# A hybrid conv/RWKV-7 layer on one core: another table of dense steps, and a y that is read from PSUM twice instead of copied

## The chip, the core and the metric

One NeuronCore of a Trainium2 chip runs the whole layer. TensorE (PE) multiplies, VectorE (DVE) and ScalarE (ACT) do the elementwise work, GpSimd (POOL) a few masks and some DMA issues, SyncE (SP) issues the other DMAs. The metric is the device time of one execution in microseconds (us); lower is better. The kernel before takes 2533.69 us (median of three runs, 2532.3 to 2533.92).

## The reference

One layer on 512 tokens and 16 meta tokens (T = 528) with width 2048, all in float32:

```
h = rms_norm(h_res, g);  p = h @ w_in
y_conv = short_conv(p[:, :3072])            # 8 tiles of 128 channels
r, k, v, decay, a, gate = token_shift(p[:, 3072:], mu), ...
S_t = S_{t-1} * w_t + (S_{t-1} a_t) b_t^T + v_t k_t^T;   y_t = S_t r_t    # per head of 64
y = (y - mean(y)) * rsqrt(var(y) + eps) * lnx_w + lnx_b
y_rwkv = (y + sum(r * k * r_k) * v) * g
h_res += concat(y_conv, y_rwkv) @ w_out
h_res += square(relu(rms_norm(h_res) @ w_up)) @ w_down
out = rms_norm(h_res)[16:]
```

## The kernel before, in words

Every large product is made of "dense steps": for one 128-row slice of the contraction, three matmuls (high part of the weights by high and low part of the activations, low part of the weights by high part). ACT casts each raw block of weights to its high part (`split`, L663), DVE subtracts to get the low part (`split`, L920); four dense steps use one such block.

The RWKV heads are worked in 8 pairs of two heads. The first seven pairs are one loop (PE L1506, ACT L820, DVE L1180), the last stands behind it. One pair has two strands that PE interleaves: 96 dense steps that make the projections of conv tiles and of the next pair's r, k, v (six tiles of 16 steps; 48 in the last pair), and the pair's own chain of small steps in chunked form. Each step of the chain has a name: ss (sum of squares of the key), low (decay and rate), vtr, gram0, tr, gram1, amv, base1 and base2 (DVE inverts 16x16 blocks, which SP carries through DRAM and back), x16, t16, x32, tt32 (the inverse is doubled), pq, gh, y0, z2 to z8 (the state is passed from chunk to chunk), y, and var. `PACE` (L70) says how many dense steps PE does ahead of each named step; `schedule` adds them up, and for the last pair caps them at 48. All three engines walk the same table: at each name ACT and DVE do that step's part (`steps_of`) and then the weight splits that are due (one per four dense steps), or, for the names in SPLIT_FIRST (L133: low, base1, base2, x16, y, var), the splits first. Engines meet by three counters (`pe_done`, `act_done`, `dve_done`); `dve("rt")` in PE's code is a wait until DVE has done its step rt.

The part that the change touches most, at a pair's end: PE's y adds the last term into PSUM banks 2 and 3 of PW. ACT squares them into ysq (sqc, L788) and copies them to SBUF (yk into ybuf, L789). PE's var puts the head means of the squares into bank 0 and the gate product into bank 1. ACT takes the square root (std, L792), DVE the reciprocal (inv2, L1133), multiplies ybuf by it (y1, L1134), applies weight and bonus (y2, L1136) and multiplies by the gate in bank 1 (y4, L1137). The next pair begins with kk on DVE (L1000), a square on ACT (sq, L742) and on PE ss (L1354), which writes banks 2 and 3 again.

Of the kernel before, what the change touches and what calls it, by code (L numbers as in the profile page):

```python
# [28 lines left out]
ALU = mybir.AluOpType  # L29
# [6 lines left out]
SEQ = 512  # L36
# [30 lines left out]

PACE = dict(ss=2, low=5, vtr=5, ahead0=6, gram0=8, tr=2, gram1=3, base1=0, base2=0, amv=2, ahead1=4, ahead2=4,  # L70
            ahead3=4, ahead4=5, ahead5=4, x16=3, t16=2, x32=2, tt32=2, pq=2, gh=3, y0=5, z2=4, z3=2, z4=1, z5=2, z6=1,
            z7=2, z8=2, y=2, var=3, ahead6=4)

PE_STEPS = [n for n in PACE if n[:4] != "base" and n[:5] != "ahead"]
Z_STEPS = ("z2", "z3", "z4", "z5", "z6", "z7", "z8")
ACT_STEPS = ["for_sqrt", "sq", "nrm", "for_sig", "sigw", "siga", "for_exp", "vtok", "epv", "em", "ep", "gs", "ghi", "btok",
             "ktok", "bonb", "atok", "mv", "x16", "x32", "warm", "pq", "sqc", "yk", "std"]
DVE_STEPS = (["kk", "ssm", "inv", "ld", "scan", "mid", "mu", "epv", "gs", "kkn", "tfac", "kp",
              "at", "b", "bt", "rt", "kt", "rb", "gram0", "bon", "glo", "gram1", "diag"]
             + [f"{s}{m}" for m in (2, 4, 8) for s in ("pr", "ar", "pl", "al")] + ["ut"]  # L80
# [25 lines left out]
def at(static, per=0, it=0):  # L106

    return it * per + static


def step(steps, name, it):

    return at(steps.index(name) + 2, len(steps), it)
# [9 lines left out]
def schedule(last):  # L123
    pace, total = [], 0
    for n in PACE.values():
        total += n
# [13 lines left out]

Y_FROM = list(PACE).index("x16")

# [21 lines left out]
def hybrid_layer(nc, x, meta, norm_mix_g, w_in, shift_mu, conv_w, decay_w0, decay_w2, iclr_a0, iclr_a2,  # L164
# [85 lines left out]
    warm = m_sb("warm", [P, 1])  # L250
    uni = m_sb("uni", [P, 9 * T])
    ld, mu, ep, em, epv, asig, kk, kp, fsq = (uni[:, i * T:(i + 1) * T] for i in range(9))
    W = SLOTS * C
# [3 lines left out]
    INV = by_chunk(0, 2).rearrange("p m c n -> p (m c) n")  # L257
    PROD_AT = 10 * W
    PQ = uni[:, 0:4 * W].rearrange("p (h c n) -> p h c n", h=2, c=SLOTS)
    ybuf = uni[:, 4 * W:4 * W + SEQ]  # L260
    ycen = uni[:, 4 * W + SEQ:4 * W + 2 * SEQ]
    low_g, low_g2 = em, epv[0:TAIL]
    ET = uni[:, 4 * W + 2 * SEQ:4 * W + 3 * SEQ]
    ysq = uni[:, 0:SEQ]
# [60 lines left out]
    def halves(ap):  # L325
        return ap.rearrange("p (a n) -> p a n", a=2)
# [8 lines left out]
    def token_order(ap):  # L335

        return ap.rearrange("p (k a n) -> p a k n", a=2, n=C)

    def by_bank(b):

        return PW[:, b:b + 2, 0:4 * C].rearrange("p a (k n) -> p a k n", n=C)

    def in_row(i):

        return PW[:].rearrange("p a n -> p (a n)")[:, i * TP:(i + 1) * TP]

    def turned(b):

        return PW[:, b:b + 2, :].rearrange("p a n -> p (a n)")[:, 0:TP]

    def pw(b):
        return PW[:, b:b + 2, 0:HALF]
# [288 lines left out]
    def _(act):  # L641
# [83 lines left out]
        def pair(j, last=False):  # L725
            n_done = [0]

            def done(name, ins):
                assert ACT_STEPS[n_done[0]] == name, (name, ACT_STEPS[n_done[0]])
                n_done[0] += 1  # L730
                ins.then_inc(act_done, 1)
                own(name)

            pe = lambda name: act.wait_ge(pe_done, step(PE_STEPS, name, j))
            dve = lambda name: act.wait_ge(dve_done, step(DVE_STEPS, name, j))
# [3 lines left out]
            def steps_of(name):  # L739
                if name == "ss":  # L740
                    done("for_sqrt", nc.scalar.activation(warm[:], eps_t[:, 0:1], ACT.Sqrt))
                    done("sq", nc.scalar.activation(fsq, zk[:], ACT.Square, scale=feat("k_k")))  # L742
                    dve("ssm")
                    done("nrm", nc.scalar.activation(fsq, fsq, ACT.Sqrt))
                    done("for_sig", nc.scalar.activation(warm[:], eps_t[:, 0:1], ACT.Sigmoid))
                if name == "low":
                    pe("low")
                    done("sigw", nc.scalar.activation(halves(ld), pw(0), ACT.Sigmoid, bias=feat("w0")))
                    done("siga", nc.scalar.activation(halves(asig), pw(2), ACT.Sigmoid, bias=feat("a0")))
                    done("for_exp", nc.scalar.activation(warm[:], eps_t[:, 0:1], ACT.Exp))  # L750
                if name == "vtr":
                    pe("vtr")
                    done("vtok", nc.scalar.copy(v_tok[:].rearrange("p c n -> p (c n)"), turned(0)))
                    dve("epv")
                    done("epv", nc.scalar.activation(epv, epv, ACT.Exp))
                    done("em", nc.scalar.activation(em, mu, ACT.Exp, scale=-1.0))
                    done("ep", nc.scalar.activation(ep[:, 0:SEQ], mu[:, META:T], ACT.Exp))
                    dve("gs")
                    done("gs", nc.scalar.activation(gs[:], gs[:], ACT.Exp))
                if name == "ahead0":  # L760
                    act.wait_ge(g_loaded, at(64, 64, j))
                    nc.scalar.copy(g_hi[:], g_w[:])
                    done("ghi", nc.scalar.copy(g_tail[:], g_w2[:]))
                if name == "tr":
                    pe("tr")
                    done("btok", nc.scalar.copy(b_tok[:].rearrange("p c n -> p (c n)"), in_row(0)))
                    done("ktok", nc.scalar.copy(k_tok[:].rearrange("p c n -> p (c n)"), in_row(1)))
                    dve("bon")
                    done("bonb", nc.scalar.activation(bonus[:], bonus[:], ACT.Identity, bias=feat("lnb")))
                if name == "amv":  # L770
                    pe("amv")
                    done("atok", nc.scalar.copy(AMV[:, :, :, 0:HS], PW[:, 2:4, 0:W].rearrange("p h (c n) -> p h c n", c=SLOTS)))
                    done("mv", nc.scalar.copy(AMV[:, :, :, HS:P], PW[:, 0:2, 0:W].rearrange("p h (c n) -> p h c n", c=SLOTS)))
                if name in ("x16", "x32"):
                    pe(name)
                    b = 2 if name == "x16" else 0
                    done(name, nc.scalar.copy(XM[:, :, 1:, :].rearrange("p h c n -> p h (c n)"), PW[:, b:b + 2, C:W]))
                if name == "tt32":

                    done("warm", nc.scalar.activation(warm[:], eps_t[:, 0:1], ACT.Sqrt))  # L780
                if name == "pq":
                    pe("pq")
                    for h in range(2):
                        ins = nc.scalar.copy(PQ[:, h, :, :].rearrange("p c n -> p (c n)"), turned(2 * h))
                    done("pq", ins)
                if name == "y":
                    pe("y")
                    done("sqc", nc.scalar.activation(token_order(ysq), by_bank(2), ACT.Square))  # L788
                    done("yk", nc.scalar.copy(token_order(ybuf), by_bank(2)))  # L789
                if name == "var":  # L790
                    pe("var")
                    done("std", nc.scalar.activation(ysq, PW[:, 0, :], ACT.Sqrt, bias=eps_t[:, 1:2]))  # L792

            splits, tiles, y_split = 0, 0, 0
            for i, (name, k) in enumerate(zip(PACE, schedule(last))):

# [96 lines left out]
    def _(dve):  # L893

        V = nc.vector
# [85 lines left out]
        def pair(j, last=False):  # L981
            n_done = [0]

            def done(name, ins):
                assert DVE_STEPS[n_done[0]] == name, (name, DVE_STEPS[n_done[0]])
                n_done[0] += 1
                ins.then_inc(dve_done, 1)
                own(name)
# [8 lines left out]
            def steps_of(name):  # L997
# [133 lines left out]
                if name == "var":  # L1131
                    act("std")
                    done("inv2", V.reciprocal(ysq, ysq))  # L1133
                    done("y1", V.tensor_tensor(ycen, ybuf, ysq, ALU.mult))  # L1134
                    act("bonb")
                    done("y2", V.scalar_tensor_tensor(ycen, ycen, feat("lnw"), bonus[:], ALU.mult, ALU.add))  # L1136
                    done("y4", V.tensor_tensor(bt[:, PAD + META:TP], ycen, PW[:, 1, :], ALU.mult))  # L1137
# [19 lines left out]
            splits, tiles, y_split = 0, 0, 0  # L1157
            for i, (name, k) in enumerate(zip(PACE, schedule(last))):
                if name not in SPLIT_FIRST:
# [112 lines left out]
    def _(pe):  # L1272
# [62 lines left out]
        def pair(j, last=False):  # L1335
            n_done = [0]

            def done(name, ins):
                assert PE_STEPS[n_done[0]] == name
                n_done[0] += 1  # L1340
                ins.then_inc(pe_done, 1)

            act = lambda name: pe.wait_ge(act_done, step(ACT_STEPS, name, j))
            dve = lambda name: pe.wait_ge(dve_done, step(DVE_STEPS, name, j))
# [5 lines left out]
            def steps_of(name):  # L1350
                if name == "ss":
                    act("sq")
                    for a in range(2):
                        ins = M(PW[:, 2 + a, 0:HALF], same_head[:], half(fsq, a), start=True, stop=True)  # L1354
                if name == "low":
# [138 lines left out]
            k_steps = 0  # L1494
            for name, k in zip(PACE, schedule(last)):
                while k_steps < k:
# [96 lines left out]
```

## Time and profile before

| | us |
|---|---|
| median of three runs | 2533.69 |
| the profiled execution | 2533.69 |
| its span | 2532.2 |
| PE busy | 2441.7 (96%) |
| DVE busy | 1133.7 (45%) |
| ACT busy | 794.5 (31%) |

The span runs from the first to the last instruction of the profiled execution, and its own time is 1.5 us longer. PE's busy time counts matmuls that overlap as one. A pair takes about 98 us, the eight stand between about 114 and 900 us. Where a row says "idle before <- X", the engine had nothing to do until X was done; "issue" means that no releaser was seen.

### The profile page before, as it was taken

Reading aid. Unit: us, or ns where it says so; the run is one execution under the profiler, and the core shown is the slowest. Engines: PE = TensorE matmul, PEld = TensorE weight load, DVE = VectorE, ACT = ScalarE, POOL = GpSimd, SP = SyncE. Lnnn points to the kernel's source line nnn. Section 1 sums busy time; section 2 is a strip of 40 time slices with the busy share of each in tenths; the row PEclk is TensorE's granted clock in tenths of the full one; section 3 lists DMA queues with packets and bytes.
Section 4 is the critical chain, followed back from the end, with each engine's and each line's share of the span. In section 5 each row is a group of like instructions: output and inputs, shape, how many; then the busy total and the mean of one; then the engine's idle time right before and its main releaser. Section 6 shows DMA issues by size and latency. Waiting matters only on the chain.

```text
span 2532.2 us, 44221 instructions
## 1 busy us (share of the span) xinstructions
PE 2441.7 (96%) x16510; PEld 2062.2 (81%) x16510; DVE 1133.7 (45%) x1725; ACT 794.5 (31%) x1333; POOL 177.2 (7%) x207
## 2 busy tenths in 40 slices
PE   6999999999999789999999999999999999999997
PEld 6988888889889568888888888888888888888886
DVE  6357566476576554443333333333333333333343
ACT  6334333344344222232232232232232222221333
POOL 4001001010010022200000000000000000000033
PEclk8999999999999889999999999999999999999999
DMA  8242432342432453333323233223333333332332
GB/s 210 75 91 74 96 88 74 93 94 67 97 84 79 107 156 93 89 94 108 92 83 108 86 88 108 87 87 108 88 102 91 89 102 91 90 100 83 100 92 92
DMA packets 507783, 242.87 MB, mean 96 GB/s; under 512 B 102976, under 2 KB 500672, under 8 KB 507136
## 3 DMA queue, kind: packets, MB, share of 16 engines
q1 hardware_dynamic: 502672, 226.63, 32.9%
q0 software_dynamic: 4992, 14.43, 1.7%
q8 instruction: 102, 1.67, 0.3%
q14 instruction: 17, 0.14, 0.0%
HBM read 224.08 MB, written 16.92 MB: 95 GB/s over the span
## 4 chain that ended last, share of the span: by engine, by line
PE 85%; DMA 5%; DVE 4%; SPq 2%; ACT 2%; issue 2%; ACTq 0%; DVEq 0%
PE PD L1320 63%; PE PD L1323 16%; DMA w_raw<-in_w_in 2%; DMA gram<-NA 1%; DMA inverse<-UU 1%; DMA UU<-gram 1%; PE PW L1429 1%; SPq L387 1%; PE PW L1474 1%; DVE uni L1082 0%; DVE w_lo L920 0%; DVE uni L1076 0%; DMA x_rows<-in_x 0%; DVE act_lo L925 0%; PE PW L1436 0%
## 5 line engine op out<-in xcount | busy, mean ns | idle before, releaser
L920 DVE TENSOR_TENSOR w_lo<-w_raw,w_hi 128x512 fp32r<-128x512 f32 x780 | 555.9, 750 | 312.9 <-ACT w_hi L663 304.9
L663 ACT CAST w_hi<-w_raw 128x512 fp32r<-128x512 f32 x780 | 455.9, 619 | 730.1 <-PE PD L1320 484.5
L1320 PE MATMUL PD<-act_hi,w_hi 128*128 128x512 f32 x1408 | 557.6, 396 | 8.3 <-DVE act_lo L978 8.3
L1320 PE MATMUL PD<-act_lo,w_hi 128*128 128x512 f32 x1408 | 558.6, 397 | 0.0
L1320 PE MATMUL PD<-act_hi,w_lo 128*128 128x512 f32 x1408 | 555.6, 395 | 0.0
L1320 PE MATMUL PD<-u_hi,w_hi 128*128 128x512 f32 x1024 | 409.7, 400 | 0.0
L1320 PE MATMUL PD<-u_hi,w_lo 128*128 128x512 f32 x1024 | 403.3, 394 | 0.0
L1320 PE MATMUL PD<-u_lo,w_hi 128*128 128x512 f32 x1024 | 401.5, 392 | 0.0
L1320 PEld LDWEIGHTS PD<-act_hi,w_hi 128*128 128x128 f32 x1408 | 265.6, 189 | 73.3 <-DVE act_lo L978 9.2
L1323 PE MATMUL PD<-act_hi,w_hi 128*128 128x264 f32 x1376 | 298.9, 299 | 20.0 <-DVE act_lo L925 10.5
L1320 PEld LDWEIGHTS PD<-act_hi,w_lo 128*128 128x128 f32 x1408 | 266.1, 189 | 60.4
L1320 PEld LDWEIGHTS PD<-act_lo,w_hi 128*128 128x128 f32 x1408 | 265.2, 188 | 60.7 <-issue 0.2
L1323 PE MATMUL PD<-act_lo,w_hi 128*128 128x264 f32 x1376 | 281.1, 286 | 0.0
L1323 PE MATMUL PD<-act_hi,w_lo 128*128 128x264 f32 x1376 | 280.8, 286 | 0.0
L1255 DVE TENSOR_TENSOR res<-PD,res 128x512 f32<-128x512 f32 x128 | 88.5, 692 | 413.6 <-PE PD L1320 413.6
L1323 PEld LDWEIGHTS PD<-act_hi,w_hi 128*128 128x128 f32 x1376 | 214.2, 190 | 36.7 <-issue 23.6
L1320 PEld LDWEIGHTS PD<-u_hi,w_lo 128*128 128x128 f32 x1024 | 192.2, 188 | 50.1
L1320 PEld LDWEIGHTS PD<-u_lo,w_hi 128*128 128x128 f32 x1024 | 192.2, 188 | 45.1
L1320 PEld LDWEIGHTS PD<-u_hi,w_hi 128*128 128x128 f32 x1024 | 192.2, 188 | 43.7
L1323 PEld LDWEIGHTS PD<-act_lo,w_hi 128*128 128x128 f32 x1376 | 214.5, 189 | 0.0
L1323 PEld LDWEIGHTS PD<-act_hi,w_lo 128*128 128x128 f32 x1376 | 214.2, 189 | 0.0
L1239 DVE SCALAR_TENSOR_TENSOR nt<-PD,rs 128x512 f32<-128x512 f32 x64 | 44.3, 692 | 366.1 <-PE PD L1320 365.9
(263 smaller groups left out, 1475.8 us busy)
## 6 DMA issues: line engine op xcount, KB each, us to landing
w_raw<-in_w_up SPq DMA_DIRECT2D x256, 256.0 KB, 3.1
w_raw<-in_w_down SPq DMA_DIRECT2D x256, 256.0 KB, 2.9
w_raw<-in_w_in SPq DMA_DIRECT2D x200, 256.0 KB, 3.4
w_raw<-in_w_out SPq DMA_DIRECT2D x64, 256.0 KB, 2.8
x_rows<-in_x SPq DMA_DIRECT2D x4, 1024.0 KB, 8.2
residual<-res POOLq DMA_DIRECT2D x2, 2048.0 KB, 12.0
out<-rows SPq DMA_DIRECT2D x8, 512.0 KB, 4.9
uni<-inverse SPq DMA_DIRECT2D x16, 240.0 KB, 4.2
```

What stands on the lines that cost most here:

```text
L387: sp.dma_start(w_raw[:, q % RAW, :, first:first + width], src).then_inc(raw_loaded[q % RAW], 16)
L663: nc.scalar.copy(w_hi[:, q % RING], w_raw[:, q % RAW]).then_inc(hi_split, 1)
L920: V.tensor_tensor(w_lo[:, q % RING], w_raw[:, q % RAW], w_hi[:, q % RING].bitcast(F32), ALU.subtract).then_inc(lo_split, 1)
L1239: V.scalar_tensor_tensor(nt1[:, m % 3, :], pd_seq(n), 0.0, rs1[:], ALU.max, ALU.mult).then_inc(evacuated[n % 2], 1)
L1255: V.tensor_tensor(res[:, m, :], pd_seq(n), res[:, m, :], ALU.add).then_inc(evacuated[n % 2], 1)
L1320: ins = M(pd_seq(n), w, v[:, k, first:first + SEQ], start=begin, stop=end)
L1323: ins = M(PD[:, 2 * (n % 2) + a, 0:HALF], w, v[:, k, a * HALF:(a + 1) * HALF], start=begin, stop=end)
L1429: ins = M(PW[r, 2 + h, k * C:(k + 1) * C], XM[r, h, k, :], TTM[r, h, k, :], start=True, stop=True)
L1474: ins = M(PW[:, (c - 1) % 2, 0:P], GT[:, c - 1, :], HB[:, 0, :] if c == 1 else ZB[:, c - 2, :], start=True, stop=True)
```

## The change

The table PACE is another one (still 96 steps in sum); ahead6, which had 4 steps behind var, is gone, and amv stands ahead of base1 and base2. In cumulative dense steps: gram0 comes at 24 (26 before), gram1 at 29 (31), amv at 31 (33), x16 at 54 (57), t16 56 (59), x32 59 (61), pq 64 (65), gh 67 (68), y0 72 (73), z2 to z8 at 76, 78, 80, 82, 84, 86, 88 (77, 79, 80, 82, 83, 85, 87), y 91 (89), var 96 (92). ACT no longer copies y (yk); y1 reads it from PSUM. PE waits for kk ahead of ss.

```diff
-PACE = dict(ss=2, low=5, vtr=5, ahead0=6, gram0=8, tr=2, gram1=3, base1=0, base2=0, amv=2, ahead1=4, ...
-            ..., z7=2, z8=2, y=2, var=3, ahead6=4)
+PACE = dict(ss=2, low=4, vtr=5, ahead0=6, gram0=7, tr=2, gram1=3, amv=2, base1=0, base2=0, ahead1=2, ...
+            ..., z7=2, z8=2, y=3, var=5)
@@ ACT_STEPS
-             "ktok", "bonb", "atok", "mv", "x16", "x32", "warm", "pq", "sqc", "yk", "std"]
+             "ktok", "bonb", "atok", "mv", "x16", "x32", "warm", "pq", "sqc", "std"]
@@
-    ybuf = uni[:, 4 * W:4 * W + SEQ]
@@ ACT, name == "y"
                     done("sqc", nc.scalar.activation(token_order(ysq), by_bank(2), ACT.Square))
-                    done("yk", nc.scalar.copy(token_order(ybuf), by_bank(2)))
@@ DVE, name == "var"
                     done("inv2", V.reciprocal(ysq, ysq))
-                    done("y1", V.tensor_tensor(ycen, ybuf, ysq, ALU.mult))
+                    done("y1", V.tensor_tensor(token_order(ycen), by_bank(2), token_order(ysq), ALU.mult))
@@ PE, name == "ss"
                     act("sq")
+                    dve("kk")
                     for a in range(2):
                         ins = M(PW[:, 2 + a, 0:HALF], same_head[:], half(fsq, a), start=True, stop=True)
```

PE at the end of the loop's body and the start of the next pair, before. The rows end with ss; PW is the PSUM of the small steps, PD that of the dense ones, and var's matmuls stand four dense steps further up:

```order
L1323 MATMUL PD<-act_hi,w_lo 128x264 x2
L1506 REGISTER_ALU
L1506 COMPARE_AND_BRANCH
L1323 MATMUL PD<-act_hi,w_hi 128x264 [waits lo_split,evacuated0]
L1323 MATMUL PD<-act_hi,w_hi 128x264
L1323 MATMUL PD<-act_lo,w_hi 128x264 x2
L1323 MATMUL PD<-act_hi,w_lo 128x264 x2
L1323 MATMUL PD<-act_hi,w_hi 128x264 x2
L1323 MATMUL PD<-act_lo,w_hi 128x264 x2
L1323 MATMUL PD<-act_hi,w_lo 128x264 x2
L1354 MATMUL PW<-uni,same_head 128x264 [waits pair_steps_act]
```

The same place on PE in the changed kernel (lines are two less, from L1353 on one less):

```order
L1488 MATMUL PW<-low_tail,g_tail 128x512
L1505 REGISTER_ALU
L1505 COMPARE_AND_BRANCH
L1321 MATMUL PD<-act_hi,w_hi 128x264 [waits lo_split,evacuated0]
L1321 MATMUL PD<-act_hi,w_hi 128x264
L1321 MATMUL PD<-act_lo,w_hi 128x264 x2
L1321 MATMUL PD<-act_hi,w_lo 128x264 x2
L1321 MATMUL PD<-act_hi,w_hi 128x264 x2
L1321 MATMUL PD<-act_lo,w_hi 128x264 x2
L1321 MATMUL PD<-act_hi,w_lo 128x264 x2
L1353 MATMUL PW<-uni,same_head 128x264 [waits pair_steps_dve,pair_steps_act]
```

The last matmul of var now stands directly ahead of the branch, and ss waits for DVE's counter as well as for ACT's.

DVE at the same place, from y4 to the first step behind ss, before:

```order
L1137 TENSOR_TENSOR bt<-uni,PW 128x512 [waits pair_steps_dve]
L993 REGISTER_ALU
L919 REGISTER_ALU [waits pair_steps_dve]
L920 TENSOR_TENSOR w_lo<-w_raw,w_hi 128x512 [waits hi_split]
L1180 REGISTER_ALU
L1180 COMPARE_AND_BRANCH
L1000 TENSOR_SCALAR uni<-zk,par 128x528 [waits z_done]
L1002 TENSOR_SCALAR uni<-PW 128x528 [waits pair_steps_pe,pair_steps_dve]
```

and now:

```order
L1135 TENSOR_TENSOR bt<-uni,PW 128x512 [waits pair_steps_dve]
L991 REGISTER_ALU
L1178 REGISTER_ALU [waits pair_steps_dve]
L1178 COMPARE_AND_BRANCH
L998 TENSOR_SCALAR uni<-zk,par 128x528 [waits z_done]
L1000 TENSOR_SCALAR uni<-PW 128x528 [waits pair_steps_pe,pair_steps_dve]
```

The weight split between y4 and the branch is gone (it stands ahead of the reciprocal), so the branch comes directly behind the wait for y4.

ACT in front of the copy that t16 waits for (L777, of PE's x16), before, from the cast of the third last block on:

```order
L662 REGISTER_ALU [waits raw_loaded3]
L663 CAST w_hi<-w_raw 128x512 [waits quarter_used]
L660 REGISTER_ALU
L662 REGISTER_ALU [waits raw_loaded0]
L663 CAST w_hi<-w_raw 128x512 [waits quarter_used]
L662 REGISTER_ALU [waits raw_loaded1]
L663 CAST w_hi<-w_raw 128x512 [waits quarter_used]
L734 REGISTER_ALU
L777 COPY uni<-PW 128x2x256 [waits pair_steps_pe]
```

and now:

```order
L661 REGISTER_ALU [waits raw_loaded3]
L662 CAST w_hi<-w_raw 128x512 [waits quarter_used]
L659 REGISTER_ALU
L661 REGISTER_ALU [waits raw_loaded0]
L662 CAST w_hi<-w_raw 128x512 [waits quarter_used]
L733 REGISTER_ALU
L776 COPY uni<-PW 128x2x256 [waits pair_steps_pe]
```

The cast of the block in raw_loaded1 has moved behind the copy.

## Rows read from the trace of the kernel before

**Rows 1.** The page: busy time of the engines, PE's granted clock in 40 slices.

```profile
PE 2441.7 (96%) x16510; PEld 2062.2 (81%) x16510; DVE 1133.7 (45%) x1725; ACT 794.5 (31%) x1333; POOL 177.2 (7%) x207
...
PEclk8999999999999889999999999999999999999999
```

**Rows 2.** Waits of PE, whole span: line, releaser, us in total, times, longest.

```profile
PE PW L1410 <- DMA uni<-inverse: 8.2, 4, 7.3
PE PW L1418 <- ACT uni L777: 7.9, 8, 1.1
PE PW L1354 <- ACT uni L742: 6.4, 8, 2.2
...
PE PW L1392 <- DVE KA L1038: 2.9, 8, 0.4
```

**Rows 3.** PE's timeline at a boundary: start, duration, instruction, [idle before <- releaser].

```profile
404.05 0.39 PE L1489 MATMUL PW<-low_tail,g_tail 128*128 128x512 f32 x1
404.28 0.40 PE L1323 MATMUL PD<-act_hi,w_hi 128*128 128x264 f32 x2
...
406.96 0.40 PE L1323 MATMUL PD<-act_hi,w_lo 128*128 128x264 f32 x2
409.12 0.50 PE L1323 MATMUL PD<-act_hi,w_hi 128*128 128x264 f32 x2 [1.76 <-issue]
...
410.43 0.40 PE L1323 MATMUL PD<-act_hi,w_lo 128*128 128x264 f32 x2
411.11 1.16 PE L1354 MATMUL PW<-uni,same_head 128*128 128x264 f32 x4 [0.28 <-ACT uni L742]
```

**Rows 4.** ACT's timeline at the same boundary.

```profile
404.48 0.69 ACT L792 ACTIVATE uni<-PW,eps_t 128x512 f32<-128x512 f32 x1 [2.23 <-PE PW L1489]
...
408.69 1.28 ACT L741 ACT_TABLE_LOAD   x1
...
410.32 0.74 ACT L742 ACTIVATE uni<-zk,par 128x528 f32<-128x528 f32 x1
```

**Rows 5.** DVE's timeline at the same boundary.

```profile
405.20 3.35 DVE L1133 RECIPROCAL uni<-uni 128x512 f32<-128x512 f32 x1 [2.23 <-ACT uni L792]
408.59 0.69 DVE L1134 TENSOR_TENSOR uni<-uni 128x512 f32<-128x512 f32 x1
409.52 0.75 DVE L1136 SCALAR_TENSOR_TENSOR uni<-uni,par,bonus 128x512 f32<-128x512 f32 x1 [0.24 <-DVE uni L1134]
410.31 0.69 DVE L1137 TENSOR_TENSOR bt<-uni,PW 128x512 f32<-128x512 f32 x1
411.12 0.69 DVE L920 TENSOR_TENSOR w_lo<-w_raw,w_hi 128x512 fp32r<-128x512 f32 x1
411.73 0.49 DVE L1000 TENSOR_SCALAR uni<-zk,par 128x528 f32<-128x528 f32 x1
```

**Rows 6.** Timelines of ACT and PE at the boundary to the last pair.

```profile
798.90 0.69 ACT L792 ACTIVATE uni<-PW,eps_t 128x512 f32<-128x512 f32 x1 [2.23 <-PE PW L1489]
...
804.01 1.16 PE L1354 MATMUL PW<-uni,same_head 128*128 128x264 f32 x4 [0.77 <-ACT uni L742]
```

**Rows 7.** Timelines of PE and ACT around x16 and t16 of one pair.

```profile
462.03 0.69 PE L1410 MATMUL PW<-uni 64*64 64x64 f32 x32 [0.36 <-DMA uni<-inverse]
...
463.45 1.37 ACT L663 CAST w_hi<-w_raw 128x512 fp32r<-128x512 f32 x2 [0.16 <-DMA w_raw<-in_w_in]
464.73 0.58 ACT L777 COPY uni<-PW 128x512 f32<-128x512 f32 x1
...
465.45 0.69 PE L1418 MATMUL PW<-uni 64*64 64x64 f32 x32 [1.06 <-ACT uni L777]
```

**Rows 8.** PE's timeline in the last pair: two of its waits.

```profile
855.04 1.13 PE L1410 MATMUL PW<-uni 64*64 64x64 f32 x32 [7.29 <-DMA uni<-inverse]
...
876.65 1.13 PE L1466 MATMUL PW<-NA,uni 64*64 64x64 f32 x32 [3.90 <-DVE uni L1125]
```

**Rows 9.** PE by stretches: length, busy, granted clock, DMA share, GB/s.

```profile
874.00:876.00 2.00, 0.00 (x0) 0.74 0.06 21
...
880.00:882.00 2.00, 2.00 (x9) 0.55 0.09 33
```

More of the change, by code:

```diff
@@ L66 @@
 ACC_STEPS = 1 + 2 * (KT - 1)
-PACE = dict(ss=2, low=5, vtr=5, ahead0=6, gram0=8, tr=2, gram1=3, base1=0, base2=0, amv=2, ahead1=4, ahead2=4,
-            ahead3=4, ahead4=5, ahead5=4, x16=3, t16=2, x32=2, tt32=2, pq=2, gh=3, y0=5, z2=4, z3=2, z4=1, z5=2, z6=1,
-            z7=2, z8=2, y=2, var=3, ahead6=4)
+PACE = dict(ss=2, low=4, vtr=5, ahead0=6, gram0=7, tr=2, gram1=3, amv=2, base1=0, base2=0, ahead1=2, ahead2=4,
+            ahead3=4, ahead4=4, ahead5=4, x16=5, t16=2, x32=3, tt32=2, pq=3, gh=3, y0=5, z2=4, z3=2, z4=2, z5=2, z6=2,
+            z7=2, z8=2, y=3, var=5)
 PE_STEPS = [n for n in PACE if n[:4] != "base" and n[:5] != "ahead"]
```

## The prediction

> **What bounds the kernel now.** I read the page first: TensorE (PE) is busy 96% of the span and the granted clock is at full in nearly every slice [rows 1]. Then the list of waits of PE alone, which says where the missing 4% goes. In the stage of the eight head pairs (114 to 900 us) it has four small entries that come back in every pair or nearly so: x16 waits for the inverse to come back by DMA (8.2 us in 4 waits), t16 waits for a copy of ScalarE (ACT) (7.9 in 8), ss waits for ACT's square (6.4 in 8), amv waits for VectorE (DVE) (2.9 in 8) [rows 2]. DVE is busy 45% and ACT 31%, but they matter wherever PE waits for a chain on them. Then the timelines of PE, ACT and DVE around the end of one pair (404 to 412 us). PE finishes the matmuls of var (last one 404.05 + 0.39 = 404.44), runs four dense steps (404.28 to about 407.2, so 0.73 us a step), stands idle 1.76 us with no releaser at the loop's branch, runs two more dense steps and starts ss at 411.11, after 0.28 us of waiting for ACT [rows 3]. ACT comes from the standard deviation (404.48), a table load (408.69) and the square (410.32, 0.74 long, so ended 411.06), which releases ss [rows 4]. DVE is later than both: reciprocal 3.35 us, y1, y2, y4 (ended 411.00), one weight split, and kk from 411.73 to 412.22 [rows 5]. So DVE's chain is off PE's path today, and ends 1.1 us behind the start of ss.
>
> **The change, part by part.**
>
> 1. *ss waits for kk.* y1 now reads banks 2 and 3 of PSUM at the end of the chain, and ss writes them, so ss has to stand behind y1; the wait is for kk, which stands behind y1, y2 and y4 on DVE. At the same time var moves from dense step 92 to 96, directly ahead of the branch, and nothing else of PE stands between var and ss but the branch and two dense steps. The start of std on ACT (404.48) is my zero, S; it follows var's last matmul by 0.04. On DVE y4 ends at S + 6.52 (411.00). The split that stood between y4 and kk goes ahead of the reciprocal, where DVE idles. kk then starts 0.12 after y4, as the split did (411.12), at S + 6.64, takes 0.49 and releases ss at about S + 7.18, with 0.05 for the release as in the row of ss [rows 3, 5]. PE gets to ss at S + 1.72 (the idle stretch of 1.76 stays, I assume, less the 0.04) + 2 x 0.73 = S + 3.2. So it stands 4.0 us. Against before: ss started at S + 6.63, and S itself now comes four steps later, 2.93 us. Cost of a boundary: 2.93 + 7.18 - 6.63 = 3.48 us. Six boundaries branch back and look like this, 20.9 us. The seventh leads to the last pair, which stands behind the loop: there ss started at 804.01 with std at 798.90, 5.11 behind it, for no table load stands in its way, so it loses 2.93 + 7.18 - 5.11 = 5.0 us [rows 6]. Sum 25.9 us. Queued behind the waiting ss on PE are all dense steps of the next pair, and PE is the bound, so nothing takes the loss back.
>  The lower bound of this term is the wait paid only on y1, as if kk and the rest came earlier: y1 ends at S + 4.80, 2.4 us less a boundary, 9 us in sum. That is not what the code waits for. The upper bound is that DVE's own branch, now bare between y4 and kk, costs what PE's does, 1.76; before, kk followed the start of the split by 0.61 with the branch between them, so it costs at most 0.61 there [rows 5]. I take 0 and keep 0.6 x 6 = 3.7.
>  The Trainium skill has a rule that speaks against this change here: in "Runtime: NRT & Kernel Launch", section "Instruction fetch mechanics", a taken branch to a target that is no longer held makes the engine fetch it by DMA before it can go on. PE's 1.76 us looks like that; DVE's branch does not in these rows. If DVE's did too, the case is the second rival below.
>
> 2. *y1 reads PSUM, yk goes.* y4 is a tensor_tensor with one operand in PSUM and takes 0.69, y1 with both in SBUF takes 0.69 [rows 5]; so 0, and as bounds the last digit of these durations, under 0.1 a pair either way. The copy yk took about 0.6 of ACT between y and var, where ACT waits anyway; bounds 0 and -0.6 us in the last pair, where ACT's next cast feeds PE. I take 0.
>
> 3. *Dense steps moved inside the pair.* PE's dense work is the same, only its place moves. (a) At gram1, one weight split of DVE falls behind KA instead of ahead of it; amv waits 2.9 / 8 = 0.36 us today, and I take 0.25 of it as gained, seven times: -1.8. (b) From gram0 to x16 there were 31 dense steps (26 to 57), now 30 (24 to 54). The round trip of the gram blocks through DRAM and DVE must fit in there. x16 waited 0.9 us in three of the seven looped pairs (8.2 less the 7.29 of the last pair), as at 462.03 [rows 2, 7, 8]. The window shrinks by 0.73 + 0.25, so the wait grows by up to 0.98, and by less where there was slack; I take 0.8, seven times: +5.6. (c) ACT's copy for t16 stood behind three casts that came late, the last two 1.37 us (463.45), and started at 464.73; t16 then waited 1.06. Now two casts stand ahead, so the copy comes about 0.6 earlier: -4.2 [rows 7]. (d) In the last pair steps are capped at 48 in both, so x16 stays there while gram0 comes two steps earlier: its wait of 7.29 us shrinks by 1.5 [rows 8]. (e) z4 and z6 get one more step and amv is written ahead of base1: no wait of the looped pairs stands there, 0. Two steps fewer from ss to gram0 (24 to 22) could bring a new wait of at most 1.46; low and vtr come 0.73 earlier too, and I take 0. Sum of part 3: -1.8 + 5.6 - 4.2 - 1.5 = -1.9. Bounds: -8 ((b) at 0) to +10 ((e) at 1.46).
>
> 4. *The clock.* Idle stretches on PE were followed by a drop of the granted clock. After the wait of 3.90 us before 876.65 the row for 874 to 876 has 0.74 and that for 880 to 882 has 0.55: half speed (1.2 GHz) from about 875.0 to 881.8, so 6.8 us [rows 8, 9]. At the pair boundaries, with 1.76 + 0.28 idle, it never dropped: the slices of the looped pairs show 9 [rows 1, 3]. The new boundary has the 1.76, two dense steps and then 4.0 idle (5.5 or so, unbroken, at the last). That is nearer to the stretch that dropped. A drop of 6.8 us lies 1 to 3 us in the idle stretch; in the other 4 to 6 us PE does half the work, so it loses 2 to 3, say 2.4. Bounds 0 and 7 x 3.4 = 24; I take a drop at five or six of seven, 13 us.
>  "TensorE: Matmul & The Clock Gate" of the Trainium skill, section "Part 1: The HAM clock gate", says that the engine falls to half rate after idleness and has to earn the full rate back by sustained work. The trace agrees for the waits named above; how it answers to a shorter gap no row shows.
>
> Sum: 25.9 - 1.9 + 13 = +37. The profiled execution took 2533.69 us (span 2532.2 and 1.5 around it), which is also the median of the three runs. Forecast: 2533.7 + 37 = 2571 us.
>
> **The rivals.**
> - *The stall without the clock.* For it: full clock through seven boundaries today. Against it: 4.0 us is longer than the 3.90 us that came before a drop. Time: 2533.7 + 25.9 - 1.9 = 2558.
> - *DVE's branch is bare and dear.* Against it the 0.61 between split and kk; for it PE's 1.76 in the same place. Its price is PE's 1.76 less the 0.12 already counted behind y4, so 1.6 at each of the six boundaries that branch: the forecast + 10 = 2581. (This is the case that the page on the runtime speaks of.)
> - *The wait is covered, and the kernel gets faster.* One mechanism: if the chain from std to kk ended before PE has done the branch and two steps, ss would neither wait for DVE nor, in the main, for ACT, and the four steps moved ahead of var would fill PE's waits: 0.6 x 7 at ss, 4.2 at t16, 1.8 at amv, 1.5 in the last pair, -12 us, 2522. It decides at 3.2 us from S. Against it: the reciprocal alone takes 3.35 [rows 5].
>
> **How the numbers follow.** Forecast 0.60, stall without the clock 0.24, dear branch 0.11, covered 0.05. The forecast's own bounds run from three cheap drops (2563) to seven dear ones (2580). The range has to take in the second case and half of the third: 2554 to 2583. 0.2% of this time is 5 us, about what a measurement of this kernel tells from no change. Only the last case is not slower; I give it 0.03 for faster, 0.02 for neither, and 0.95 for slower.
>
> **What would show it.** On PE, ss waits for DVE's kk at each of seven boundaries, about 4.0 us six times and 5 to 6 once; the entry "ss waits for ACT" is gone; ss starts 7.2 us behind std. t16's wait falls to about 0.4, x16's grows to about 1, and the last pair's to 5.8. Granted clock of half for some 7 us behind most boundaries; if it stays full, part 4 is wrong and the time is near 2558. If ss waits under 1 us, part 1 is wrong, and with it the sign.

## The result, and the profile after

The changed kernel takes 2576.82 us (median of four runs, 2574.91 to 2578.06) against 2533.81 beside it: a ratio of 1.0169, interval 1.0151 to 1.0186, slower by about 43 us. The forecast was 2571, range 2554 to 2583. The profiled execution took 2576.31 us with a span of 2574.8, 42.6 longer than before.

The waits of PE over the whole span, as in [rows 2] (line, releaser, us in total, times, longest):

```profile
PE PW L1353 <- DVE uni L998: 36.8, 7, 6.0
PE PW L1409 <- DMA uni<-inverse: 12.9, 8, 4.0
...
PE PW L1417 <- ACT uni L776: 3.1, 7, 0.8
...
PE PW L1353 <- ACT uni L741: 2.3, 1, 2.3
PE PW L1381 <- DVE NA L1036: 1.3, 7, 0.2
...
PE PW L1377 <- DVE ar L1030: 1.2, 7, 0.2
```

The first row is new: ss now waits for kk seven times, 5.3 us each on average. t16's wait (L1417) has shrunk from 7.9 to 3.1, x16's (L1409) has grown outside the last pair from 0.9 to 8.9, in the last pair it has gone from 7.3 to 4.0, and amv's wait for KA is gone. The one wait of ss for ACT that is left (2.3 us) is that of the first pair.

PE at a boundary of two pairs, the answer to [rows 3] (start, duration, instruction, [idle before <- releaser]):

```profile
420.80 0.39 PE L1488 MATMUL PW<-low_tail,g_tail 128*128 128x512 f32 x1
422.02 0.50 PE L1321 MATMUL PD<-act_hi,w_hi 128*128 128x264 f32 x2 [0.84 <-issue]
...
423.35 0.40 PE L1321 MATMUL PD<-act_hi,w_lo 128*128 128x264 f32 x2
428.90 2.13 PE L1353 MATMUL PW<-uni,same_head 128*128 128x264 f32 x4 [5.15 <-DVE uni L998]
...
450.58 1.31 PE L1377 MATMUL PW<-ar,bt 64*64 64x128 f32 x36 [0.18 <-DVE ar L1030]
```

var, branch, two dense steps, then 5.15 us of nothing. ss itself takes 2.13 us instead of 1.16, since the clock has dropped (rows below), and gram0, which never waited before, now waits 0.18 us for DVE as well.

ACT and DVE at the same boundary, for [rows 4, 5]:

```profile
421.22 0.69 ACT L790 ACTIVATE uni<-PW,eps_t 128x512 f32<-128x512 f32 x1 [3.77 <-PE PW L1488]
...
421.94 3.35 DVE L1131 RECIPROCAL uni<-uni 128x512 f32<-128x512 f32 x1 [3.69 <-ACT uni L790]
425.33 0.69 DVE L1132 TENSOR_TENSOR uni<-PW,uni 128x512 f32<-128x512 f32 x1
426.26 0.75 DVE L1134 SCALAR_TENSOR_TENSOR uni<-uni,par,bonus 128x512 f32<-128x512 f32 x1 [0.24 <-DVE uni L1132]
427.04 0.69 DVE L1135 TENSOR_TENSOR bt<-uni,PW 128x512 f32<-128x512 f32 x1
428.35 0.49 DVE L998 TENSOR_SCALAR uni<-zk,par 128x528 f32<-128x528 f32 x1 [0.62 <-DVE bt L1135]
...
846.22 0.49 DVE L998 TENSOR_SCALAR uni<-zk,par 128x528 f32<-128x528 f32 x1 [0.22 <-DVE bt L1135]
```

From std (S = 421.22) to ss it is 7.68 us; the forecast had 7.18. y1 takes 0.69 from PSUM as it did from SBUF. The last row is the boundary to the last pair, where DVE has no branch to take: kk follows y4 by 0.22 there and by 0.62 to 0.66 at the other six. By that difference DVE's bare branch costs 0.4 us.

The clock around this boundary (stretch: length, PE busy, granted clock, DMA share, GB/s):

```profile
424.00:426.00 2.00, 0.00 (x0) 1.00 0.00 0
426.00:428.00 2.00, 0.00 (x0) 0.53 0.00 0
428.00:430.00 2.00, 1.10 (x3) 0.50 0.25 94
430.00:432.00 2.00, 2.00 (x9) 0.50 0.33 89
432.00:434.00 2.00, 2.00 (x15) 0.77 0.02 5
```

It falls to half (1.2 GHz) while PE is idle, at 426.1 by these rows, and is back at 432.9, 6.8 us later; PE works in 4.0 of them. The trace has a drop at each of the seven boundaries, 6.8 us long at five and 3.4 at two, and each begins while PE stands idle ahead of ss.

### The profile page after: what moved, and what is told of

It reads as the page before. It is cut to its first block, busy times and chain, and to the rows that moved or that the text cites. A ratio compares the mean times of both kernels' runs of the same rounds, so it can differ in the third digit from the quotient of the medians.

```text
span 2574.8 us, 44179 instructions
## 1 busy us (share of the span) xinstructions
PE 2455.0 (95%) x16510; PEld 2076.1 (81%) x16510; DVE 1134.2 (44%) x1725; ACT 789.6 (31%) x1325; POOL 177.6 (7%) x207
## 4 chain that ended last, share of the span: by engine, by line
PE 84%; DVE 7%; DMA 3%; ACT 2%; issue 2%; SPq 1%; DVEq 0%; ACTq 0%
PE PD L1318 62%; PE PD L1321 14%; DMA w_raw<-in_w_in 1%; DVE uni L1131 1%; DMA inverse<-UU 1%; PE PW L1428 1%; PE PW L1353 1%; DVE uni L1080 0%; DVE uni L1074 0%; PE PW L1473 0%; PE PW L1377 0%; DMA uni<-inverse 0%; DVE act_lo L923 0%; PE PW L1435 0%; SPq L439 0%
## 5 line engine op out<-in xcount | busy, mean ns | idle before, releaser
L1318 PEld LDWEIGHTS PD<-act_hi,w_hi 128*128 128x128 f32 x1408 | 265.7, 189 | 72.0 <-DVE act_lo L976 8.6
L1321 PE MATMUL PD<-act_hi,w_hi 128*128 128x264 f32 x1376 | 305.0, 304 | 14.5 <-DVE act_lo L923 9.2
L1321 PEld LDWEIGHTS PD<-act_hi,w_hi 128*128 128x128 f32 x1376 | 220.3, 195 | 31.9 <-issue 21.2
```

The source lines that it names most:

```text
L1318: ins = M(pd_seq(n), w, v[:, k, first:first + SEQ], start=begin, stop=end)
L1321: ins = M(PD[:, 2 * (n % 2) + a, 0:HALF], w, v[:, k, a * HALF:(a + 1) * HALF], start=begin, stop=end)
```

## The experiments

Times stand beside runs of the kernel before on the same chip, 2535 to 2537 us. Differences to the changed kernel are those of the medians; its own runs were taken beside others of the kernel before, and by the ratios the 17, 20 and 22 us below are 18, 19 and 25. For the traces I use three distances: from std to ss and from ss to gram0, averaged over the seven boundaries, and from gram0 to x16, averaged over the seven looped pairs.

**The table alone.** The kernel before with only its table replaced:

```diff
-PACE = dict(ss=2, low=5, vtr=5, ahead0=6, gram0=8, ... y=2, var=3, ahead6=4)
+PACE = dict(ss=2, low=4, vtr=5, ahead0=6, gram0=7, ... y=3, var=5)
```

> The new table alone: ACT copies y as before, y1 reads the copy, and ss does not wait for kk. Theory A (var moved next to the branch puts DVE's chain on the path, with or without the wait): ss waits for ACT's square only and starts about 4.5 us behind std, but DVE cannot begin the next pair's chain before kk has ended at 7.6 us behind std, so PE waits at gram0 instead, some 2 us a pair. About 2.7 us a pair against before, less 2: 2551 us (2545 to 2557), granted clock mostly full at the boundaries. Theory B (the added wait for kk is the whole loss, the table by itself is a small gain): 2530 to 2534 us. The prediction on record has nothing for this kernel apart from its part 3 (-2 us) and the 2.9 us of the four steps moved.

Measured: 2551.19 us, ratio 1.0065 (1.0048 to 1.0081). Two rows of PE:

```profile
417.33 1.16 PE L1354 MATMUL PW<-uni,same_head 128*128 128x264 f32 x4 [1.93 <-ACT uni L742]
...
438.90 1.31 PE L1378 MATMUL PW<-ar,bt 64*64 64x128 f32 x36 [1.82 <-DVE ar L1032]
```

As theory A has it: ss starts 4.5 us behind std at the six boundaries with a branch (2.98 at the last), and the rest comes back at gram0, which waits 1.8 us for DVE (1.0 at the last). The table costs 16 us without any wait for kk. In this trace the clock stays up at all seven boundaries; it drops once in the looped pairs behind them, at 238.2, just behind one of these waits of gram0. Theory B falls.

**The wait alone.** The changed kernel with the old table:

```diff
-PACE = dict(ss=2, low=4, vtr=5, ahead0=6, gram0=7, ... y=3, var=5)
+PACE = dict(ss=2, low=5, vtr=5, ahead0=6, gram0=8, ... y=2, var=3, ahead6=4)
```

> The old table with y1 reading PSUM, no copy yk, and ss waiting for kk. Theory A: kk ends 7.74 us behind std (the split stands between y4 and kk), ss starts at 7.8 instead of 6.63 and 5.11: +1.2 us at six boundaries and +2.7 at the last, 2544 us without a drop of the clock, up to 2552 with one at most boundaries (idle 1.76 and 1.45 us with two dense steps between; I think it stays full). Theory B: the wait brings most of the +43 us by itself, 2570 or more.

Measured: 2549.34 us, 1.0059 (1.0043 to 1.0076).

```profile
413.04 0.51 PE L1321 MATMUL PD<-act_hi,w_hi 128*128 128x264 f32 x2 [1.62 <-issue]
416.33 1.16 PE L1353 MATMUL PW<-uni,same_head 128*128 128x264 f32 x4 [1.56 <-DVE uni L998]
```

ss comes 7.8 us behind std, as expected, and from ss to gram0 it is 21.1 at five boundaries; at the other two, 23.1 and 22.6, the clock has dropped. The time lies between the 2544 expected without a drop and the 2552 with one at most boundaries. So the two halves cost 16.5 and 15 us by their ratios, 31 together, and the whole change 43. The other 11 or so (the intervals leave it open by some 7) are there only when both halves are. They fit the clock (theory C of the next run), which stays up at most boundaries with either half and drops at all seven with both. The traces bear it out. From std to gram0 the kernel before takes 27.48 us. At full clock, and counting the 2.93 us of the steps moved ahead of std, the table alone takes 1.34 us more a boundary, the wait alone 1.41, and both together 2.87 (in *The filler earlier*, below): so far the halves simply add. The seven drops of the changed kernel cost 14.4 us from ss to gram0, the two of this run 3.6, and the table alone has none there.

**Work for PE in the gap.** The changed kernel with filler matmuls:

```diff
                 if name == "ss":
                     act("sq")
+                    for _ in range(12):
+                        M(PW[:, 0, :], low_hi[:, 0:P], low_hi[:], start=True, stop=True)
                     dve("kk")
```

> The changed kernel with 12 extra matmuls of 512 columns (about 2.6 us at full clock, result never read) on PE between the wait for ACT's square and the wait for kk, where PE stands idle. ss still starts 7.7 us behind std. Theory C (the dropped clock behind each boundary costs about 2.0 us a boundary): the granted clock stays full there, and the time falls by 14 us less the 2.6 that the first pair pays: 2565 us (2561 to 2570). Rival D (the 2 us between ss and gram0 are DVE's chain alone and the clock costs nothing): 2577 to 2580 us.

Measured: 2559.69 us, 1.0098 (1.0081 to 1.0115), 17 us less than the changed kernel, though PE does more, and a little below the expected range. The distance from ss to gram0 falls from 21.8 to 19.7 us, as expected of the clock; what was not foreseen is that gram0 to x16 falls as well, from 29.6 to 28.4 (see the next run). But the clock still drops at four boundaries, between 0.2 us ahead of the filler's start and 0.9 behind it:

```profile
419.00:421.00 2.00, 0.79 (x7) 1.00 0.00 0
421.00:423.00 2.00, 1.11 (x3) 0.68 0.00 0
423.00:425.00 2.00, 2.00 (x6) 0.50 0.00 0
```

There the filler runs at half speed and outlasts kk, so that ss starts 8.9 us behind std. Hence the next one.

**The filler earlier.** Against the run before, there are 17 matmuls, and they begin once ACT has done the step ahead of its square (for_sqrt):

```diff
-                    act("sq")
-                    for _ in range(12):
+                    act("for_sqrt")
+                    for _ in range(17):
                         M(PW[:, 0, :], low_hi[:, 0:P], low_hi[:], start=True, stop=True)
+                    act("sq")
                     dve("kk")
```

> As e3_filler, but 17 matmuls that begin as soon as ACT has finished the step ahead of its square, about 3.6 us behind std, so that PE stands idle for some 1.2 us less before them. Theory C (what is left of the loss of clock in e3_filler comes from the idle time ahead of the filler): no drop at the pair boundaries but the first, 2 to 5 us less than e3_filler's 2559.7, so 2556 us (2553 to 2560). Rival: the drops come for another reason and stay, 2560 or more.

Measured: 2556.43 us, 1.0093 (1.0078 to 1.0108), and no drop at any of the seven boundaries.

```profile
417.87 4.15 PE L1352 MATMUL PW<-low_hi 128*128 128x512 f32 x17 [1.18 <-ACT warm L740]
421.91 1.16 PE L1356 MATMUL PW<-uni,same_head 128*128 128x264 f32 x4
441.74 1.31 PE L1380 MATMUL PW<-ar,bt 64*64 64x128 f32 x36 [0.18 <-DVE ar L1030]
```

```profile
417.00:419.00 2.00, 1.14 (x5) 1.00 0.00 0
419.00:421.00 2.00, 2.00 (x11) 1.00 0.00 0
421.00:423.00 2.00, 2.00 (x10) 1.00 0.24 90
```

ss starts 7.7 us behind std as in the changed kernel, so the stall is the same; from ss to gram0 it is 19.8 us, against 21.8. The run *The inside of the pair alone*, which has the new steps and no filler, also shows 19.81 us at the five boundaries that branch back with a full clock. So the drops cost 2.05 us each on average (1.3 to 2.7), 14.4 us in sum.

The whole difference to the changed kernel is 20 us. From gram0 to x16 it is 28.35 us here and 29.6 in the changed kernel, 8.8 us over the seven looped pairs. Against it stands the filler ahead of the first pair's ss, which hides behind nothing and costs 3.7 us. The 8.8 us are the landing of the last inverse load that x16 waits for: it is issued 23.7 us behind gram0 here and 23.6 there, but takes 4.4 us to land instead of 5.9. DMA around this load in one pair, first the changed kernel (474 to 480 us), then this run (465 to 471):

```profile
q8 instruction: 1, 0.02, 1.5%
...
uni<-inverse SPq DMA_DIRECT2D x1, 80.0 KB, 5.9
```

```profile
q1 hardware_dynamic: 3738, 1.21, 110.6%
issues: line engine op xcount, KB each, median us to landing
...
uni<-inverse SPq DMA_DIRECT2D x1, 80.0 KB, 4.4
```

In the changed kernel a block of the program itself (queue "instruction", 16 KB) is loaded inside that window; in this run the window has none. The ten traces have 80 such loads. In 56 such a block begins while the load is under way: 53 of these take 4.9 to 6.5 us, and the other three, whose blocks begin late (2.9 to 3.5 us behind the issue), take 4.4 to 4.7. The 24 without one, which are all those of both filler runs and of every last pair, take 4.1 to 4.7. So this part of the gain goes with where the code blocks fall, which the extra matmuls shift, and not with the clock. That the block is what delays the load is the plain reading; no run moves the blocks alone.

**A wait for y1 only.** ss waits for the last reader of its banks, by a counter of its own:

```diff
                     done("y1", V.tensor_tensor(token_order(ycen), by_bank(2), token_order(ysq), ALU.mult))
+                    dve.sem_inc(banks_read, 1)
@@ PE, name == "ss"
-                    dve("kk")
+                    pe.wait_ge(banks_read, at(1, 1, j))
```

> The changed kernel, but ss waits for y1, the last reader of the banks, through a counter of its own, and no longer for kk. Theory A: ss starts about 5.0 us behind std instead of 7.7; ssm on DVE starts right behind kk, at about 8.2, instead of at 9.8, so gram0 comes about 1.6 to 2.1 us earlier a boundary, plus the clock's 2.0 where it no longer drops: 2550 to 2562 us, and PE waits at gram0 for DVE. Theory B: the whole of the wait is given back, 2.7 us a boundary and the clock, 2544 us or less, with no new wait at gram0.

Measured: 2555.12 us, 1.0072 (1.0056 to 1.0089), 22 us less than the changed kernel by the medians.

```profile
419.35 1.16 PE L1356 MATMUL PW<-uni,same_head 128*128 128x264 f32 x4 [2.68 <-DVEq L1134]
...
440.58 1.31 PE L1380 MATMUL PW<-ar,bt 64*64 64x128 f32 x36 [1.59 <-DVE ar L1031]
```

ss starts 4.9 us behind std, 2.8 earlier, but at this boundary gram0 then waits 1.6 us for DVE: part of what is not waited for at ss is waited for there. The clock still drops at five of seven boundaries, so the total does not say what the wait alone gives back. The two boundaries with a full clock do: from std to gram0 they take 26.15 us, against 27.5 in *The filler earlier*, also at full clock. Waiting for kk and not only for y1 costs 1.3 to 1.4 us a boundary, half of the 2.8.

**The inside of the pair alone.** The kernel before with the new steps from low to z5, but y at 89, var at 92, four steps behind it, and no new wait:

```diff
-PACE = dict(ss=2, low=5, vtr=5, ahead0=6, gram0=8, ... z4=1, z5=2, z6=1,
+PACE = dict(ss=2, low=4, vtr=5, ahead0=6, gram0=7, ... z4=2, z5=2, z6=1,
             z7=2, z8=2, y=2, var=3, ahead6=4)
```

> The kernel before with the new table from low to z5 (gram0 at 24, x16 at 54, amv ahead of base1), but the end of the pair as it was: y at 89, var at 92, four steps behind it, the copy yk, no wait for kk. This is part 3 of the prediction by itself: -1.9 us, bounds -8 to +10, so 2533 us against 2535. If it comes out beyond +5, the inside of the pair holds a part of the loss that I gave to the boundary; if beyond -5, part 1 and the clock together cost more than I said.

Measured: 2535.63 us against 2537.09, ratio 0.9996 (0.9987 to 1.0005). Inside the pair the change is worth nothing measurable, and the forecast's -1.9 lies inside this interval. The trace also says whose the longer waits of x16 are: 6.9 us in the looped pairs here, 0.9 in the kernel before, with the clock up at six of the seven boundaries. They come with the steps and need no drop of the clock.

**PE's small waits, taken away.** Two edits of the kernel before. First only ACT's order at x16:

```diff
-                if name not in SPLIT_FIRST:
+                splits_first = name in SPLIT_FIRST and name != "x16"
+                if not splits_first:
                     steps_of(name)
```

> The kernel before, with one edit: at x16 ACT makes the copy that t16 waits for ahead of the weight casts that are due, not behind them. If t16's wait (7.9 us in 8) is only ACT's order, it goes and nothing replaces it: -7 us, 2528 us. Rival: the casts behind the copy are late for DVE's splits and PE waits for weights a few steps on: no change.

Measured: 2529.76 us, 0.9982 (0.9973 to 0.9991), 4.6 us less by the ratio, where 7 were expected. t16's wait fell from 7.9 to 2.4, not to nothing. Then with ss, x16 and one of DVE's splits moved as well:

```diff
-PACE = dict(ss=2, low=5, ... x16=3, t16=2, x32=2,
+PACE = dict(ss=3, low=4, ... x16=4, t16=2, x32=1,
@@ DVE
-                while splits < k // KQ:
+                while splits < k // KQ and name != "tr":
```

> As e6_copy_first, with ss one dense step later (3 and 4 instead of 2 and 5), DVE's weight split that is due at tr moved behind the KA of gram1, and x16 one step later (4, 2, 1 instead of 3, 2, 2). Takes away the waits of ss for ACT (-4 us), of amv for DVE (-2.5) and of x16 for the DMA (-0.9, or it comes back as +0.3 a pair) on top: 2520 to 2523 us. Rival: the waits of the chain move on to gram0 or x16 one for one, and it ends at e6_copy_first's time.

Measured: 2520.25 us, 0.9946 (0.9933 to 0.9960). This is the best version, 14 us below the kernel before, and inside the expected 2520 to 2523. From the list of PE's waits now, where ss for ACT and t16 each stand once, with 1.5 and 0.8 us:

```profile
PE PD L1324 <- issue: 9.6, 6, 1.9
...
PE PW L1411 <- DMA uni<-inverse: 5.2, 1, 5.2
...
PE PD L1324 <- DVE w_lo L921: 3.5, 6, 0.7
```

The waits of x16, t16 and ss have all but gone from the looped pairs, and amv's is down to 0.2 us in one; a wait for weights (3.5 us) has come in their place. The idle time at the branch is what stays. The three moves that this run adds were not run apart, so their shares are not known.

## Why the prediction was right

1. *ss waits for kk.* Right in place and mechanism. Std to ss is 7.68 to 7.72 us six times and 7.37 once (7.18 forecast). With the four steps of 2.93 us that is 4.0 a boundary and 5.2 at the last, 29.1 us in sum against 25.9. The missing 0.5 is 0.4 for DVE's branch, which I had taken at 0 with a bound of 0.61, and 0.1 because kk follows y4 by 0.22 even without a branch, not by the 0.12 of the split. The dear branch, the second rival, is out: 0.4 us, not 1.6. What PE's own branch shows as idle time, 0.5 to 1.2 here, only shifts time into the wait behind it. The term stands on a deeper cause than the step named: with var next to the branch DVE's chain is late for the whole next pair, and the table alone shows it as a wait at gram0. The wait for kk adds 1.3 to 1.4 us a boundary to it, because ss, and everything of DVE behind ss, starts later still.
2. *y1 from PSUM, yk gone.* 0, as forecast: y1 takes 0.69 in both, and before, ACT stood idle for 2.23 us ahead of std [rows 4], so the copy held nothing up there. What the copy is worth in the last pair no run takes apart.
3. *Steps moved in the pair.* -1.9 forecast. By the waits of the two traces: x16 +8.0 in the looped pairs (forecast 5.6), the last pair -3.3 (-1.5), t16 -4.8 (-4.2), amv -2.9 (-1.8), and small new waits of 0.18 each at gram0 and tr, +2.5. Sum -0.5. The kernel that has only these steps measures the same as before. That the sum came out so near is in part luck: the misses (+2.4, -1.8, -0.6, -1.1, and +2.5 that I had at 0) cancel in the main. The last pair gained more than the two steps (1.5), because the last inverse load also lands 2.0 us sooner behind gram0 there.
4. *The clock.* 13 us forecast, as 2.4 us at five or six boundaries. It dropped at all seven and cost 2.05 each, 14.4: too few drops and too high a price, which nearly cancel. The Trainium skill ("TensorE: Matmul & The Clock Gate", section "Part 1: The HAM clock gate") has it that idleness drops the clock and sustained work raises it again; here it fell with PE idle at all seven boundaries and came back while PE worked. The forecast's own upper bound of 2580 does not fit its 24 us for seven dear drops, which give 2582.

29.1 - 0.5 + 14.4 = 43.0, and the spans differ by 42.6. So close a match is luck too. The sum leaves out a drop in the first pair (at 115.5, about 1.6 us from ss to gram0), one in the middle of a pair (at 374.9, about 1.0 us), and PE's waits for act_lo, which fell by 1.7 us in sum; about 1 us is not accounted for. The first rival (no clock) is refuted by the granted clock at all seven boundaries and by the filler runs, the second by DVE's 0.4 us, the third (covered) by every row of the boundary. What stays open is why the clock dropped at some boundaries and not at others like them (below).

## What to carry to other kernels

When work is moved away from behind a step, ask what that work was hiding: here four dense steps covered a chain of reciprocal, y1, y2 and y4 on another engine, and a saved copy of 0.6 us on an idle engine bought nothing that shows. A wait on the engine that is the bound is paid twice if the clock drops with it. An experiment that adds instructions also moves the code: look at where its blocks are loaded before the whole gain is put down to the work added. And a busy engine's small waits are worth looking at one by one: four edits of order, none of which removes work, gave 14 us.

## What the runs showed that I had not expected

- The clock also dropped behind shorter idle stretches than the 3.90 us of [rows 8]: at four boundaries of the first filler run, where PE had stood 0.60 to 0.95 and 1.88 to 2.24 us with two dense steps between. At full clock stayed another boundary of the same run, with 0.94 and 1.90, and all six of the table alone, with 0.34 to 0.90 and 1.93 to 2.49. Likewise it dropped once each in three other runs behind 1.77 to 1.83 us at the branch, where 1.90 left it up elsewhere. So the lengths of the gaps alone don't decide it, and what does is open. With the filler earlier (0.40 to 0.96 and 1.01 to 1.57) it stayed up everywhere.
- DVE's branch back cost 0.4 us (0.62 against 0.22). PE's idle time at its own branch came out between 0.34 and 1.23 us in the kernels with var next to it, and between 1.32 and 1.91 in those with four dense steps between.
- Extra matmuls made a kernel that is bound by PE faster by 17 to 20 us, some 9 of them with the code blocks that no longer load beside x16's last DMA.
